# Modulation weights of a two-layer decoder trunk: two chunks up front, three folded through the mixer, one beside the second expert table

## The reference, cut to what matters

```
for l in range(DEPTH):
    mod = jax.nn.silu(c) @ ada_w[l] + ada_b[l]
    sh1, sc1, g1, sh2, sc2, g2 = jnp.split(mod[:, None, :], 6, axis=-1)
    h = rmsnorm(x, norm1_g[l]) * (1.0 + sc1) + sh1
    x = x + g1 * hybrid_mixer(h, positions, rel_bias, ...)
    h = rmsnorm(x, norm2_g[l]) * (1.0 + sc2) + sh2
    x = x + g2 * peer_ffn(h, ...)
```

## Time and profile before

| | us |
|---|---|
| median of three runs (2330.95 to 2333.8) | 2330.95 |
| the profiled execution, its own time | 2331.92 |
| its span, core 0 | 2330.1 |
| TensorE busy in the span | 2155.0 (92%) |
| first projection of the mixer starts at | 127.73 |
| layer 0's second table, from its first row | 857.75 |

### The profile page before, as it was taken

How to read it: one execution, slowest core, us unless ns; L and a number is a source line. 1 busy time by engine, 2 the same in 40 slices (tenths; PEclk the granted TensorE clock), 3 DMA queues, 4 the chain that set the end, 5 groups by cost and what they waited for, 6 DMA issues and landing times.

```text
span 2330.1 us, 39430 instructions
## 1 busy us (share of the span) xinstructions
PE 2155.0 (92%) x13500; PEld 1948.3 (84%) x13500; DVE 1545.6 (66%) x3026; ACT 1229.2 (53%) x2330; POOL 439.4 (19%) x184
## 2 busy tenths in 40 slices
PE   5788779999999999999998877999999999999998
PEld 4677668999999988888877766899999998888886
DVE  7669436993577867777766943699347886555555
ACT  8622424555688854444442242445468885454553
POOL 0000016889300000000000001678930000000000
PEclk9789789999999999999999977999999999999999
DMA  7733034455444447777763303445544444556553
GB/s 257 264 100 100 28 129 136 154 181 172 144 136 144 142 142 259 263 266 256 266 223 106 100 28 109 132 154 182 170 140 145 139 137 131 195 191 194 193 191 107
DMA packets 103474, 378.78 MB, mean 163 GB/s; under 512 B 11488, under 2 KB 11872, under 8 KB 102880
## 3 DMA queue, kind: packets, MB, share of 16 engines
q1 hardware_dynamic: 102672, 373.74, 48.0%
q10 hardware_dynamic: 720, 4.00, 0.4%
HBM read 375.46 MB, written 2.23 MB: 162 GB/s over the span
## 4 chain that ended last, share of the span: by engine, by line
PE 65%; issue 14%; POOL 9%; DVE 7%; ACT 2%; DMA 2%; POOLq 0%; SPq 0%; DVEq 0%; ACTq 0%
PE bank L1626 30%; POOL split_lo L478 9%; PE bank L1529 7%; PE bank L1530 7%; PE bank L1531 7%; PE bank L1593 5%; PE bank L1318 3%; DMA ring<-stream 2%; PE bank L1281 1%; PE bank L1492 1%; PE bank L1292 1%; PE bank L1343 1%; DVE grid L841 1%; DVE grid L974 1%; PE bank L1616 1%
## 5 line engine op out<-in xcount | busy, mean ns | idle before, releaser
L1529 PE MATMUL bank<-h_hi,split_hi 128*128 128x256 f32 x2304 | 670.1, 291 | 40.6 <-DVE h_lo L1080 21.3
L1530 PE MATMUL bank<-h_lo,split_hi 128*128 128x256 f32 x2304 | 655.8, 285 | 0.0
L1531 PE MATMUL bank<-h_hi,split_lo 128*128 128x256 f32 x2304 | 655.8, 285 | 0.0
L1529 PEld LDWEIGHTS bank<-h_hi,split_hi 128*128 128x128 f32 x2304 | 445.5, 193 | 47.3 <-issue 24.4
L1184 DVE TENSOR_TENSOR split_lo<-ring,split_hi 128x1024 fp32r<-128x1024 f32 x248 | 303.9, 1225 | 257.8 <-ACT w_hi L759 257.8
L478 POOL TENSOR_TENSOR split_lo<-ring,split_hi 128x1024 fp32r<-128x1024 f32 x168 | 432.6, 2599 | 186.8 <-ACT split_hi L671 186.7
L758 ACT ACTIVATE split_hi<-ring 128x1024 fp32r<-128x1024 f32 x248 | 263.2, 1061 | 359.0 <-PE bank L1626 359.0
L1530 PEld LDWEIGHTS bank<-h_lo,split_hi 128*128 128x128 f32 x2304 | 446.3, 194 | 0.0
L1531 PEld LDWEIGHTS bank<-h_hi,split_lo 128*128 128x128 f32 x2304 | 445.5, 193 | 0.0
L671 ACT ACTIVATE split_hi<-ring 128x1024 fp32r<-128x1024 f32 x296 | 298.6, 1051 | 211.8 <-PE bank L1531 211.7
L1626 PE MATMUL bank<-split_hi,w_hi 128*128 128x512 f32 x1024 | 316.9, 391 | 0.0
(11 more groups left out here) (274 smaller groups left out, 2548.6 us busy)
## 6 DMA issues: line engine op xcount, KB each, us to landing
ring<-stream SPq DMA_DIRECT2D x658, 512.0 KB, 3.3
ada_ring<-stream SPq DMA_DIRECT2D x48, 512.0 KB, 4.1
spill<-tables ACTq DMA_DIRECT2D x1, 1152.0 KB, 5.3
tables<-spill ACTq DMA_DIRECT2D x1, 1152.0 KB, 7.3
xT<-x_in SPq DMA_DIRECT2D x1, 1024.0 KB, 9.7
s5raw<-s5w ACTq DMA_DIRECT2D x2, 512.0 KB, 5.6
y_out<-hT SPq DMA_DIRECT2D x1, 1024.0 KB, 3.9
KM<-mixc SPq DMA_DIRECT2D x1, 576.0 KB, 8.0
```

Source lines behind the costliest of these rows:

```text
L1529: mm(dst, hi, x_hi, start=start, stop=False, skip_group_check=not group)
L1530: mm(dst, hi, x_lo, start=False, stop=False, skip_group_check=not group)
L1531: return mm(dst, lo, x_hi, start=False, stop=stop, skip_group_check=not group)
```

## The change

It changes where the six chunks of layer 0 are folded, and how the bias diagonals are built.

- Sixteen blocks (chunks sh1 and sc1) are folded at the start. Two masks of the bias follow each fold, and the 31 masks have a buffer each. The positions and constants are loaded ahead of the ring, x, the small columns and `mixc` behind its first four blocks.
- The diagonals of buckets 0, 3, 6, ... (11 of 31) stay on ScalarE, the other 20 buckets are built by GpSimd, with two 128 x 512 products each, in two buffers. TensorE does `ada_sums` of the first chunk after bucket 14 and of the second after bucket 21. ScalarE squares x between its diagonals.
- VectorE norms x and then works out the rotary angles. ScalarE takes their sine and copies the bias table after `hT`; TensorE waits for that copy before its first projection.
- Chunks g1, sh2 and sc2 (24 blocks) come through a ring of three slots: 12 folds after the S5 angles, 4 ahead of the latent queries, 8 in the attention, two behind each of the first four maxima. SyncE issues their loads between those of the mixer's blocks. TensorE sums the three chunks before the last `turn(5)` of the attention.
- Chunk g2 is folded beside layer 0's second table, ahead of the six of layer 1: seven turns of 16 rows instead of six of 20, with the folds at the steps `j` with `j - 2` in `(0, 2, 4, 6, 8, 10, 12, 13)`.

```diff
-ADA_TURNS = (0, 2, 4, 6, 9, 11, 13, 15)
+ADA_TURNS = (0, 2, 4, 6, 8, 10, 12, 13)
+FIRST_ADA = 2 * KT
+MIX_ADA = 3 * KT
+SKIP = ADA - FIRST_ADA
+TURN = 16
+LATE_ADA = ADA // KT + 1
+PRE_STEPS = 12
+MIX_SLOTS = 3
...
+        ge = at_byte("ge", 88 * KB + 4 * 16384, [BUCKETS - 1, P + T], F32R)
+        diagA = at_byte("diagA", 56 * KB, [2, HEADS, 2, P], F32R)
+        diagP = at_byte("diagP", 72 * KB, [2, HEADS, 2, P], F32R)
+        mix_ring = at_byte("mix_ring", 36 * KB, [MIX_SLOTS, BLOCK])
+        mix_acc = [at_byte(f"mix_acc{c}", at * KB, [BLOCK]) for c, at in enumerate((64, 72, 76))]
...
+        def by_act(b):
+            return b % 3 == 0
+        POOL_BUCKETS = [b for b in range(BUCKETS - 1) if not by_act(b)]
+        ACT_BUCKETS = [b for b in range(BUCKETS - 1) if by_act(b)]
...
             sp.dma_start(V[:, :], vec).then_inc(vec_in, 16)
+            sp.dma_start(posi, pos).then_inc(pos_in, 16)
+            sp.dma_start(K[:, :], consts).then_inc(const_in, 16)
             for s in range(RING):
                 sp.dma_start(ring[:, s, :], stream[s]).then_inc(slot_filled[s], 16)
-                if s == 1:
-                    sp.dma_start(K[:, :], consts).then_inc(const_in, 16)
-                    sp.dma_start(posi, pos).then_inc(pos_in, 16)
-                    sp.dma_start(S[:, :, :], small).then_inc(small_in, 16)
+            sp.dma_start(xT[:, :, :], x_in).then_inc(x_loaded, 16)
+            sp.dma_start(S[:, :, :], small).then_inc(small_in, 16)
             sp.dma_start(KM[:, :], mixc).then_inc(mixc_in, 16)
...
+            def fetch_mod(k):
+                if k >= MIX_SLOTS:
+                    sp.wait_ge(ada_used, FIRST_ADA + k - MIX_SLOTS + 1)
+                sp.dma_start(mix_ring[:, k % MIX_SLOTS, :], stream[FIRST_ADA + k]).then_inc(mix_filled[k % MIX_SLOTS], 16)
...
+            for j in range(FIRST_ADA):
+                sp.wait_ge(ada_used, j + 1)
+                fetch_first(RING + j)
+            for k in range(MIX_SLOTS):
+                fetch_mod(k)
+            mods_at = {2: (3, 4), 3: (5, 6, 7), 4: (8, 9, 10, 11), 7: (12, 13, 14), 20: range(15, MIX_ADA)}
+            for j in range(MIX):
+                sp.wait_ge(block_used, j + 1)
+                fetch_first(FIRST_ADA + RING + j)
+                for k in mods_at.get(j, ()):
+                    fetch_mod(k)
             for l in range(DEPTH):
-                segment(mix_at(l) + RING, MIX, block_used, l * MIX)
+                if l:
+                    segment(mix_at(l) + RING, MIX, block_used, l * MIX)
...
+                def turn(i, at, source, used):
+                    for j in range(TURN):
+                        sp.wait_ge(v_ready, i * TURN + (l * KEYS + SPLIT + at + j + 1))
+                        fetch(i * TURN + (late + RING + at + j), (late + RING + at + j) % RING)
                         if j in ADA_TURNS:
                             k = ADA_TURNS.index(j)
-                            sp.wait_ge(ada_used, i * 8 + (ADA + k - 1))
-                            sp.dma_start(ada_ring[:, k % 2, :], stream[bass.ds(i * 8 + (N_MAIN + l * ADA + k), 1)]
+                            sp.wait_ge(ada_used, i * KT + (used + k - 1))
+                            sp.dma_start(ada_ring[:, k % 2, :], stream[bass.ds(i * KT + (source + k), 1)]
                                          .rearrange("o p c -> (o p) c")).then_inc(ada_filled[k % 2], 16)
-                segment(late + RING + 120, LATE - 120, v_ready, l * KEYS + SPLIT + 120)
+                turn(0, 0, FIRST_ADA + MIX_ADA, FIRST_ADA + MIX_ADA)
+                with sp.Fori(0, ADA // KT, 1) as i:
+                    turn(i, TURN, N_MAIN + l * ADA, ADA)
+                segment(late + RING + LATE_ADA * TURN, LATE - LATE_ADA * TURN, v_ready, l * KEYS + SPLIT + LATE_ADA * TURN)
...
+            pool.wait_ge(const_in, 16)
+            pool.wait_ge(dist_ready, 1)
+            for n, b in enumerate(POOL_BUCKETS):
+                if n >= 2:
+                    pool.wait_ge(bucket_added, POOL_BUCKETS[n - 2] + 1)
+                for part, d in enumerate((drel_hi[:, :].bitcast(F32), drel_lo)):
+                    step = d[:, b * HEADS:b * HEADS + HEADS].rearrange("p (x y) -> p y x", x=2).unsqueeze(3).broadcast_to([P, 2, 2, P])
+                    last = gp.tensor_tensor(diagP[:, n % 2, :, part, :].rearrange("p (y x) c -> p y x c", y=2),
+                                            ident.unsqueeze(1).unsqueeze(1).broadcast_to([P, 2, 2, P]), step, ALU.mult)
+                last.then_inc(pool_diag, 1)
...
+            def diagonals(n):
+                b = ACT_BUCKETS[n]
+                if n >= 2:
+                    act.wait_ge(bucket_added, ACT_BUCKETS[n - 2] + 1)
                 for q in range(HEADS):
                     for part, d in enumerate((drel_hi[:, :].bitcast(F32), drel_lo)):
-                        last = nc.scalar.activation(diag[:, j, q, part, :], ident, ACT.Copy, scale=d[:, bass.ds(b * HEADS + PERM[q], 1)])
-                last.then_inc(diag_ready, 1)
-            for b in range(3):
-                if b == 2:
-                    act.wait_ge(bucket_added, 1)
-                diagonals(b, b % 2)
-            with act.Fori(0, (BUCKETS - 4) // 2, 1) as i:
-                for j in range(2):
-                    act.wait_ge(bucket_added, i * 2 + (2 + j))
-                    diagonals(i * 2 + (3 + j), (3 + j) % 2)
-            act.wait_ge(rope_arg, 1)
-            nc.scalar.activation(rope[:, :, :], kw, ACT.Sin).then_inc(rope_sin, 1)
-            act.wait_ge(bucket_added, BUCKETS - 1)
-            for q in range(HEADS):
-                at = VEC_AT["rel"][0] + PERM[q]
-                nc.scalar.activation(t5[:, q, :], bank[:, 2 + q, 0:P + T], ACT.Identity, bias=V[:, at:at + 1]).then_inc(t5_ready, 1)
+                        last = nc.scalar.activation(diagA[:, n % 2, q, part, :], ident, ACT.Copy,
+                                                    scale=d[:, b * HEADS + PERM[q]:b * HEADS + PERM[q] + 1])
+                last.then_inc(act_diag, 1)
+            for n in range(2):
+                diagonals(n)
+            act.wait_ge(x_loaded, 16)
+            squares(x_loaded, -1)
+            act.wait_ge(small_in, 16)
+            act.dma_start(s5raw[:, :], s5w[0]).then_inc(s5w_in, 16)
+            nc.scalar.activation(dt5, small_of(0, "ldt"), ACT.Exp).then_inc(s5_exp, 1)
+            for n in range(2, 5):
+                diagonals(n)
+            root(0, "ss1", D, rstd)
+            for n in range(5, len(ACT_BUCKETS)):
+                diagonals(n)
             for l in range(DEPTH):
...
+                if l == 0:
+                    act.wait_ge(rope_arg, 1)
+                    nc.scalar.activation(rope[:, :, :], kw, ACT.Sin).then_inc(rope_sin, 1)
+                    act.wait_ge(bucket_added, BUCKETS - 1)
+                    for q in range(HEADS):
+                        at = VEC_AT["rel"][0] + PERM[q]
+                        nc.scalar.activation(t5[:, q, :], bank[:, 2 + q, 0:P + T], ACT.Identity, bias=V[:, at:at + 1]).then_inc(t5_ready, 1)
...
+            def fold(acc, b, k, used):
+                if k == 0:
+                    ins = v.tensor_scalar(acc, b, siluc[:, 0:1], None, ALU.mult)
+                else:
+                    dve.wait_ge(ada_used, used)
+                    ins = v.scalar_tensor_tensor(acc, b, siluc[:, k:k + 1], acc, ALU.mult, ALU.add)
+                ins.then_inc(ada_used, 1)
+            for b in range(4):
+                reached(b)
             dve.wait_ge(silu_ready, 2)
+            for n in range(FIRST_ADA):
+                dve.wait_ge(slot_filled[n % RING], 16 * (n // RING + 1))
+                fold(g(ACC0 + n // KT * BLOCK, BLOCK), ring[:, n % RING, :], n % KT, n)
+                for b in range(4 + 2 * n, min(6 + 2 * n, BUCKETS - 1)):
+                    reached(b)
+            def mix_step(n):
+                dve.wait_ge(mix_filled[n % MIX_SLOTS], 16 * (n // MIX_SLOTS + 1))
+                fold(mix_acc[n // KT][:, :], mix_ring[:, n % MIX_SLOTS, :], n % KT, FIRST_ADA + n)
...
+            dve.wait_ge(ada_columns, FIRST_ADA // KT)
+            add_biases(0, 0, FIRST_ADA, bank[:, 7, 0:FIRST_ADA])
...
+                if l == 0:
+                    normed(l, "ss1")
+                    rope_arguments()
...
+                if l == 0:
+                    dve.wait_ge(bucket_added, BUCKETS - 1)
+                    for n in range(PRE_STEPS):
+                        mix_step(n)
+                    dve.wait_ge(rope_sin, 1)
+                    for i in range(3):
+                        last = v.tensor_scalar(rope[:, i, :], rope[:, i, :], const("mul")[:, i:i + 1], None, ALU.mult)
+                    last.then_inc(rope_ready, 1)
...
+                if l == 0:
+                    for n in range(PRE_STEPS, PRE_STEPS + 4):
+                        mix_step(n)
...
+                    if l == 0 and n < 4:
+                        for m in (2 * n, 2 * n + 1):
+                            mix_step(PRE_STEPS + 4 + m)
```

(84 more changed lines are left out.)

128 lines of the change are left out of this document (34 added, 94 removed).

## The result

The change makes the kernel slower: 2379.24 us median (2375.74 to 2381.02, four runs) against 2330.95 (2329.82 to 2333.8, four runs), a ratio of 1.0203 with an interval of 1.0186 to 1.0221. The forecast was 2365, the range 2335 to 2385: the medians differ by 48.3 us where 34 were forecast. The profiled execution took 2375.74 us with a span of 2373.9; before, the span was 2330.1.

The account below looks back on a forecast made before the run. The prediction took the kernel as bound by TensorE's order of products (busy 92% of the span). Start -31, mixer +17.5 and second table +47 gave +33.5 on 2331.92, 2365.4; with the median 1.0 lower, 2365, range 2335 to 2385.

Parts of the forecast that it names:

- The start, GpSimd takes VectorE's time: Start: VectorE and GpSimd wait for each other at a shared port; first projection at 97 instead of 127.7, -31.
- The mixer's first twelve folds: Mixer: loads chained on three slots make VectorE late; coefficient product 35 to 37 us after the first projection, 8.5 lost.
- the later folds: Mixer: the 4 folds ahead of the latent queries cost nothing, the 8 in the attention 4 us.
- The 48 column products: End of the mixer: on TensorE ahead of the last `turn(5)`, 5.1 to 8.1 less a gap of 1.6, say 5.
- The second table, the path from row 15: Layer 0's second table: TensorE idles 4.2 us a turn until the eighth fold, behind row 15's buffer, ends; stage +47.
- Loads don't bind: Second table: 24 blocks in 52 us are fewer per us than 28 in 56.1, so loads don't limit it.
- The clock: Second table: after each pause TensorE runs 4.7 us at half speed, which costs 2.3 us a turn.
- GpSimd is not free: Denies a rival for the start: port without effect on masks and folds, first projection at 72 (-56), 2340; 10%.
- The stall is not short: Denies a rival: clock stays up, mixer hides half its folds, -31 + 10 + 31 = +10, 2341; 18%.
- the worse case: Start, mixer and turns: GpSimd's broadcast operands cost more or blocks arrive late, 2375 to 2395; 14%.
- The faster case: Second table: eighth fold in time, row 15's chain doesn't hold TensorE; -31 + 17.5 + 2 = -12, 2319; 8%.

Follow-up runs that it names:

- the run without folds: Kernel after the change, but layer 0's mixer neither loads nor folds its 24 blocks (sums set to zero, column products stay): 2359.51 us in one run.
- the four buffers: Kernel after the change, with four buffers instead of two for blocks folded beside layer 0's second table, loads issued one or two rows earlier: 2375.79 us, ratio 1.0185.

## Why the prediction was right, and where its sizes were off

The sum was -31 + 17.5 + 47 = +33.5; measured were -41.8, +23.7, +64.9 and -3.0 of the rest. The direction and the main mechanism are shown. The total was 10.3 us short against the profiled execution and 14.2 against the median, because an error of 10.8 in the start was outweighed by 24.1 in the other two terms, less the 3.0. That the total is no further off than this is luck: two errors went against each other.

- **The start, GpSimd takes VectorE's time**: right in kind, shown by the run with all diagonals on ScalarE. The size was not. I charged 32 products at 1.1 us each in full, 33.2 after the overlap; VectorE lost 24.9, that is 0.78 a product. I had expected folds of about 2.3 us; they took 1.67 on average. Fold 16 ended near 59.9 instead of 70, and what follows took 26.0 us where I had 27. The cost of a 128 x 512 product was right (mostly 1.15 us in the timeline; I took 1.2). GpSimd waits too: eight of the 32 took 1.48 to 2.02 us, those of 2.02 beside a fold. Why a product costs VectorE less than its length is open; no run took it apart.
- **The mixer's first twelve folds**: the coefficient product at 35 to 37, it came at 38.7. Loads took 4.9 us from issue to landing (median) instead of 3.7, and SyncE's own blocks were late once: TensorE stood 3.71 us for a ring block at 123.78, where I had said they land just in time. The term of 8.5 was 12.2 by the run without folds; the later folds, 4 in the sum, were 4.7.
- **The 48 column products**: 5 in the sum, 8.3 measured on the path (10.2 less what TensorE had stood there before). I priced them between 0.11 and 0.17 us; they ran at 0.21. The granted clock was 0.50 from 255 us on, in the attention before them, and stayed there through the 10 us of sums, with TensorE busy throughout.
- **The second table, the path from row 15**: right, 4.2 us of pause against 4.33 in every turn whose blocks came in time; with the fold two rows earlier the pause is gone and with it 58 us.
- **Loads don't bind**: wrong by 0.56 us a turn, shown by the four buffers. In three of seven turns the last block was late, up to a pause of 6.20.
- **The clock**: I took the rows behind a pause at half speed for 4.7 us, 2.3 a turn; measured 2.4. But I left the sums, which stand first in that stretch, at their full-clock 1.68. They took 3.57, and that makes 7 x 1.9 = 13 us of the 17.9 that this term was short. Late blocks are 4 of it, the rest is about 1.
- **Rivals**: GpSimd is not free (masks 0.99 against 0.41). The stall is not short and the clock does fall. The median, 2379.24, is above the 2350 to 2378 that I gave the forecast and inside the 2375 to 2395 of the worse case. Part of what that case names came true: blocks were late, in the mixer and in three turns. GpSimd's products were not dearer. The faster case decides just where it was put, at the fold's end against the last row: moved by two rows it gives 2321.01, against 2319.

## What to carry to other kernels

When a loop's body is shortened, look at the last step that another engine does for it: the time from the last buffer set free to that step's end must still fit inside the rows that remain, or the consumer stands once a turn. A short pause of TensorE costs more than itself, since what comes next runs at half the clock, the small products in front above all: here 4.87 us of pause cost 4.2 more, and 2.5 us cost 3.6 more. So the echo shrinks far less than the pause, and the price of the first work behind the pause has to be taken at the low clock too. And an idle stretch of VectorE in front of a chain is only free for as much work as can be there in time: count the slots and the load time, not the gap.

## What the runs showed of the hardware that was not expected

- A pause of 2.19 us was enough for the low clock behind it (sums 3.57 us), where the pauses of the earlier trace rows were 4.40 and 4.49. Behind 1.82 us, in the last turn of the same run, the sums were hardly slower (1.94) and the clock fell in the rows behind them.
- One-column products don't hold the clock up: with TensorE busy throughout it fell from 1.00 to 0.50 within 96 of them in the kernel before, and stayed at 0.50 through 48 in the kernel after. Sixteen in a row behind dense work left it at 1.00 (1.84 us).
- Useless products in the pause made the kernel 21.8 us faster, with the granted clock at 1.00 throughout.
- A 128 x 384 mask from one float input went from 0.41 us to 0.99 on average beside GpSimd's products, relatively more than a fold with two inputs of 1024 (1.28 to 1.67).
